# A gated linear recurrence in three passes of hi and lo weights instead of full fp32 matmuls, with its decay taken from an exponential

## The reference, cut to what matters

```python
def rglru_block(x, w_in, conv_w, conv_b, w_r, b_r, w_i, b_i, lam, w_out):
    gate, xr = jnp.split(x @ w_in, 2, axis=-1)
    xp = jnp.pad(xr, ((0, 0), (CONV_W - 1, 0), (0, 0)))
    xc = conv_b + sum(xp[:, k:k + S] * conv_w[k] for k in range(CONV_W))
    r = jax.nn.sigmoid(block_diagonal(xc, w_r) + b_r)     # 16 blocks of 80
    i = jax.nn.sigmoid(block_diagonal(xc, w_i) + b_i)
    log_a = -LRU_C * r * jax.nn.softplus(-lam)
    a = jnp.exp(log_a)
    u = jnp.sqrt(-jnp.expm1(2.0 * log_a)) * (i * xc)
    _, h = lax.associative_scan(_linear_recurrence_combine, (a, u), axis=1)
    return (h * jax.nn.gelu(gate)) @ w_out
```

## Time and profile before

| | |
|---|---|
| median of 3 runs | 1677.28 us (1676.93 to 1679.06) |
| the profiled execution | 1676.15 us |
| its span in the trace | 1674.4 us |
| granted TensorE clock, mean | 0.979 |
| PE busy | 1585.8 us, 95% |
| DVE, ACT busy | 778.7 us (47%), 505.6 us (30%) |
| instructions | 21914 |

### The profile page before, as it was taken

How to read it: one execution, slowest core, us unless ns; L and a number is a source line. 1 busy time by engine, 2 the same in 40 slices (tenths; PEclk the granted TensorE clock), 3 DMA queues, 4 the chain that set the end, 5 groups by cost and what they waited for, 6 DMA issues and landing times.

```text
span 1674.4 us, 21914 instructions
## 1 busy us (share of the span) xinstructions
PE 1585.8 (95%) x9206; PEld 1167.3 (70%) x9206; DVE 778.7 (47%) x1028; ACT 505.6 (30%) x573; POOL 61.4 (4%) x104
## 2 busy tenths in 40 slices
PE   8997999999999998999998899999999997899997
PEld 7745433333333337999896699998999986689997
DVE  1585411111111116545656665446554566574545
ACT  1241100000000003343354244343433435434332
POOL 2000000000000000000000000000000000000000
PEclk9997999999999999999999999999999998999999
DMA  9405899999999999753223369534854222179500
GB/s 312 142 1 245 362 414 428 429 428 429 428 428 429 429 395 369 253 193 108 76 72 131 126 225 365 189 127 150 284 194 152 100 69 83 51 273 348 182 0 26
DMA packets 149473, 395.27 MB, mean 236 GB/s; under 512 B 9458, under 2 KB 109936, under 8 KB 136608
## 3 DMA queue, kind: packets, MB, share of 16 engines
q1 hardware_dynamic: 146672, 385.67, 61.3%
q0 software_dynamic: 2736, 8.68, 1.5%
HBM read 393.28 MB, written 1.05 MB: 235 GB/s over the span
## 4 chain that ended last, share of the span: by engine, by line
PE 69%; DMA 14%; DVE 10%; issue 3%; ACT 3%; POOL 1%; SPq 0%; POOLq 0%; DVEq 0%; ACTq 0%
PE bank L1424 28%; DMA ring<-in_moe_w_dram 14%; PE bank L1437 12%; PE bank L894 8%; PE bank L650 3%; PE bank L923 2%; PE bank L703 2%; PE bank L1378 2%; PE bank L1453 1%; PE bank L911 1%; PE bank L1976 1%; PE bank L943 1%; PE bank L689 1%; DVE stats L545 1%; DVE x_tok L543 1%
## 5 line engine op out<-in xcount | busy, mean ns | idle before, releaser
L894 PE MATMUL bank<-ring,arena 128*64 128x512 f32 x928 | 228.3, 596 | 9.4 <-DMA ring<-in_moe_w_dram 9.4
L1424 PE MATMUL bank<-x_hi,split_u_hi 128*128 128x256 f32 x656 | 185.9, 283 | 0.0
L1424 PE MATMUL bank<-x_lo,split_u_hi 128*128 128x256 f32 x656 | 185.6, 283 | 0.0
L1424 PE MATMUL bank<-x_hi,split_u_lo 128*128 128x256 f32 x656 | 185.6, 283 | 0.0
L1424 PE MATMUL bank<-x_hi,split_g_lo 128*128 128x256 f32 x640 | 181.1, 283 | 0.0
L1424 PE MATMUL bank<-x_lo,split_g_hi 128*128 128x256 f32 x640 | 181.1, 283 | 0.0
L1424 PE MATMUL bank<-x_hi,split_g_hi 128*128 128x256 f32 x640 | 181.1, 283 | 0.0
L894 PEld LDWEIGHTS bank<-ring,arena 128*64 128x64 f32 x928 | 69.9, 137 | 145.6 <-issue 111.8
L1282 DVE TENSOR_TENSOR split_g_lo<-ring,split_g_hi 128x2048 fp32r<-128x2048 f32 x44 | 100.8, 2292 | 112.3 <-ACT split_g_hi L1276 112.3
L1124 DVE SCALAR_TENSOR_TENSOR arena<-arena,work 128x256 f32<-128x256 f32 x32 | 15.5, 484 | 287.7 <-PE bank L943 287.6
L1424 PEld LDWEIGHTS bank<-x_hi,split_u_hi 128*128 128x128 f32 x656 | 125.8, 192 | 0.5
(11 more groups left out here) (356 smaller groups left out, 2522.2 us busy)
## 6 DMA issues: line engine op xcount, KB each, us to landing
ring<-in_moe_w_dram SPq DMA_DIRECT2D x92, 2048.0 KB, 19.1
ring<-in_ffn_w_in_dram SPq DMA_DIRECT2D x88, 1024.0 KB, 8.9
ring<-in_ffn_w_out_dram SPq DMA_DIRECT2D x44, 1024.0 KB, 8.6
ring<-in_ml_w_in_dram SPq DMA_DIRECT2D x12, 1024.0 KB, 5.2
ring<-in_rec_w_in_dram SPq DMA_DIRECT2D x10, 1024.0 KB, 13.8
ring<-in_at_w_in_dram SPq DMA_DIRECT2D x6, 1024.0 KB, 5.2
ring<-in_rec_w_out_dram SPq DMA_DIRECT2D x5, 1024.0 KB, 9.9
gb_row<-in_ln_g_dram POOLq DMA_DIRECT2D x8, 512.0 KB, 6.9
```

The source lines that it names most:

```text
L894: i = nc.tensor.matmul(bank[4 + p][64 * j:64 * j + 64, :], xe[p][:, k, :], unit_view(n, 4)[:, k % 4, :], start=(k == 0), stop=(k == KT - 1))
L1424: i = nc.tensor.matmul(up_bank(kind, s_)[:, m * T:(m + 1) * T], w, xp_[b][:, k, :], start=(k == 0 and j == 0), stop=(k == KT - 1 and j == 2))
```

## The change

- **Three passes.** Unit 0 of `rec_w_in` stays fp32. The other 9, and the 5 of `rec_w_out`, are split to hi (ACT, L233 of the changed kernel) and lo (DVE, L238): 14 splits. x is split to `rx_hi`, `rx_lo`, and the rows of each group to `ry_hi` (ACT) and `ry_lo` (DVE).
- **Ring.** A unit that is split takes two slots, the second for its hi part. So the last three `rec_w_in` loads wait for `recA_used`, and the first expert's loads wait for it too instead of for `ln_in`.
- **Decay.** A new exponential of -2 times the old argument gives the decay less the reciprocal: DVE has no L824, L825 any more, and makes the decay and the root from the exponential by two scalar_tensor_tensor operations and one tensor_scalar.
- **Memory.** The transposed x is in `x_parts` at first, so half of the zeroing of `x_parts` comes after the first unit.
- Semaphores of the memory and attention layers are merged, and their counts shifted; nothing else of these layers changes.

```diff
@@ def columns(g, o), rec_pe
                 for k in range(KT):
-                    i = nc.tensor.matmul(o[:, b * T:(b + 1) * T], unit_view(n, KT)[:, k, b * P:(b + 1) * P],
-                                         xT[:, k, :], start=(k == 0), stop=(k == KT - 1))
+                    if g == 0:
+                        i = nc.tensor.matmul(to, w_in[:, k, at], xq[:, k, :], start=(k == 0), stop=(k == KT - 1))
+                        continue
+                    nc.tensor.matmul(to, w_hi[:, k, at], rx_hi[:, k, :], start=(k == 0), stop=False)
+                    nc.tensor.matmul(to, w_hi[:, k, at], rx_lo[:, k, :], start=False, stop=False)
+                    i = nc.tensor.matmul(to, w_lo[:, k, at], rx_hi[:, k, :], start=False, stop=(k == KT - 1))
...
-                pe.wait_ge(landed[n % RING], 16 * (n // RING + 1))
-                pe.wait_ge(r["y"], g + 1)
+                n = rec_out(g)
+                pe.wait_ge(w_lo_done, 2 * GROUPS + g)
+                pe.wait_ge(rec_lo_done, 3 + g)
@@ sync_program
+            for g in range(3 * GROUPS):
+                n = rec_in(g) if g < 2 * GROUPS else rec_out(g - 2 * GROUPS)
...
-                if n >= RING:
-                    sp.wait_ge(recA_used, n - RING + 1)
+                free_for(n)
...
                 sp.dma_start(dst, src).then_inc(landed[n % RING], 16)
+                if g > 0:
+                    free_for(n + 1)
+                    sp.sem_inc(landed[(n + 1) % RING], 16)
@@ rec_act
+            rec_split_act(act, 0)
+            rec_split_act(act, 1)
             for g in range(GROUPS):
...
+                for i in ((2,), (3, 4), (5,), (6, 7), ())[g]:
+                    rec_split_act(act, i)
...
+            rec_split_act(act, 8)
             for g in range(GROUPS + 2):
...
+                    if g < 2:
+                        rec_split_act(act, 9 + g)
+                if g >= 3:
+                    rec_y_act(act, g - 3)
                 if g >= 2:
...
+                        nc.scalar.activation(rec_b[q % 2][:, b, :], th_r[q % 2][:, b, :], ACT.Exp,
+                                             scale=lam_q[:, 4, nb:nb + 1], bias=lam_q[:, 4, nb:nb + 1])
...
-                    nc.scalar.activation(root[q % 2], th_r[q % 2], ACT.Sqrt).then_inc(r["sqrt"], 1)
+                    nc.scalar.activation(root[q % 2], th_r[q % 2], ACT.Sqrt, scale=0.25).then_inc(r["sqrt"], 1)
+                    if g < GROUPS:
+                        rec_split_act(act, 9 + g)
+            rec_y_act(act, GROUPS - 1)
+        def rec_y_act(act, q):
+            act.wait_ge(r["y"], q + 1)
...
+            nc.scalar.activation(ry_hi[q][:], gelu[:, 2 * q:2 * q + 2, :], ACT.Copy).then_inc(rec_hi_done, 1)
@@ rec_dve
+                    rec_split_dve(dve, 8 + g)
+                if g == GROUPS:
+                    rec_split_dve(dve, 13)
+                if g >= 3:
+                    rec_y_dve(dve, g - 3)
                 if g >= 2:
...
-                    own.then(nc.vector.tensor_scalar(rec_b[s], th_r[s], 1.0, None, ALU.add))
-                    own.then(nc.vector.reciprocal(rec_b[s], rec_b[s]))
...
-                    own.then(nc.vector.tensor_tensor(root[s], root[s], rec_b[s], ALU.mult))
-
-                    own.then(nc.vector.tensor_scalar(rec_b[s], rec_b[s], 2.0, -1.0, ALU.mult, ALU.add))
+                    own.did(nc.vector.scalar_tensor_tensor(out=root[s], in0=rec_b[s], scalar=1.0, in1=root[s],
+                                                           op0=ALU.add, op1=ALU.mult))
+                    own.then(nc.vector.scalar_tensor_tensor(out=th_r[s], in0=rec_b[s], scalar=1.0, in1=th_r[s],
+                                                            op0=ALU.add, op1=ALU.mult))
+                    own.did(nc.vector.tensor_scalar(th_r[s], th_r[s], -1.0, 1.0, ALU.mult, ALU.add))
```

More of the change, by code:

```diff
@@ L189, in build, with rec_hi, rec_lo, rec_split_act @@
         lam_q = sb("lam_q", [P, 12, CH])
+        xq = x_parts[:, 0:KT * T].rearrange("p (k t) -> p k t", k=KT)
+        rx_hi = nc.alloc_sbuf_tensor_at("rx_hi", [P, KT, T], F32R, offset=parts_at - KT * T * 4)
+        rx_lo = nc.alloc_sbuf_tensor_at("rx_lo", [P, KT, T], F32R, offset=h_at)
+        ry_lo = nc.alloc_sbuf_tensor_at("ry_lo", [P, CH, T], F32R, offset=arena_at + 8720 * 4)
+        ry_at = (work_at, arena_at + 11280 * 4, arena_at, arena_at + 520 * 4, work_at)
+        ry_hi = [nc.alloc_sbuf_tensor_at(f"ry_hi{q}", [P, 2, T], F32R, offset=at) for q, at in enumerate(ry_at)]
+        rec_hi_done, rec_lo_done = sem("rec_hi_done"), sem("rec_lo_done")
+        w_hi_done, w_lo_done = sem("w_hi_done"), sem("w_lo_done")
+        REC_W = 3 * GROUPS - 1
+        REC_SPLITS = [rec_in(g) for g in range(1, 2 * GROUPS)] + [rec_out(g) for g in range(GROUPS)]
+        def rec_hi(n):
+            return ring_r[:, (n + 1) % RING, :]
+        def rec_lo(n):
+            return ring_r[:, n % RING, :]
+        def rec_split_act(act, i):
+            n = REC_SPLITS[i]
+            act.wait_ge(landed[n % RING], 16 * (n // RING + 1))
+            act.wait_ge(landed[(n + 1) % RING], 16 * ((n + 1) // RING + 1))
+            nc.scalar.activation(rec_hi(n), unit(n), ACT.Copy).then_inc(w_hi_done, 1)
+        def rec_split_dve(dve, i):
+            n = REC_SPLITS[i]
+            dve.wait_ge(w_hi_done, i + 1)
+            nc.vector.tensor_tensor(rec_lo(n), unit(n), rec_hi(n).bitcast(F32), ALU.subtract).then_inc(w_lo_done, 1)
         mo = {n: sem("moe_" + n) for n in (
@@ L259, in sync_program, with free_for @@
                 sp.dma_start(x_tok[:, t, :], A["x"][0, t * P:(t + 1) * P, :]).then_inc(s_x, 16)
[L261 to L262 removed]
+            def free_for(n):
+                if n >= R0 + RING:
+                    sp.wait_ge(*rec_used(n - RING))
+            for slot in range(R0):
+                sp.sem_inc(landed[slot], 16)
+            for g in range(3 * GROUPS):
+                n = rec_in(g) if g < 2 * GROUPS else rec_out(g - 2 * GROUPS)
+                if g == 2 * GROUPS:
                     sp.wait_ge(s_wzero, 1)
@@ L731, in rec_act @@
                 act.wait_ge(s_xT0, b + 1)
-                nc.scalar.activation(xT[:, 2 * b:2 * b + 2, :], bank[b][:].rearrange("p (a t) -> p a t", a=2), ACT.Copy).then_inc(s_xT0b, 1)
+                nc.scalar.activation(xq[:, 2 * b:2 * b + 2, :], bank[b][:].rearrange("p (a t) -> p a t", a=2), ACT.Copy).then_inc(s_xT0b, 1)
+            act.wait_ge(s_xT0b, 4)
+            for j in range(2):
+                nc.scalar.activation(rx_hi[:, 4 * j:4 * j + 4, :], xq[:, 4 * j:4 * j + 4, :], ACT.Copy).then_inc(rec_hi_done, 1)
+            rec_split_act(act, 0)
+            rec_split_act(act, 1)
             for g in range(GROUPS):
```

176 lines of the change are left out of this document (105 added, 71 removed).

## The result

Over 20 executions of each, the changed kernel takes 1681.38 us (1677.47 to 1683.89) and the kernel before 1677.99 (1676.78 to 1679.26): ratio 1.0018, 95% interval 1.0011 to 1.0024, **3.4 us slower**. I forecast 1678.3 and held 1672 to 1686. A second series, of seven executions, gave 1681.63 against 1677.11, ratio 1.0027 (1.0015 to 1.0038). So the time lies in the range and the sign is right, but the difference is 3.4 to 4.5 us where I forecast 1.0: small, clear of the noise, and on the edge of what I had called "within 0.2%" or just past it.

A forecast was written before the change was run, and what follows sets the result against it. PE bounds the recurrent part before the change; afterwards late gates(0) and ACT-DVE turns do. Mark shift -2.6, half clock +2.9 on gates(0) and +0.7 on project 4 sum to +1.0 us: 1678.3 us, range 1672 to 1686.

The forecast's parts named there:

- within 0.2%: Outcome class for the whole kernel: a difference up to 3.4 us, not told from no change; chance 0.49.
- PE's saving of 17.9 us: Recurrent layer: nine rec_w_in units and five projects in three passes save 10.5 + 7.4 us if PE stays the bound.
- the two places named: Gates(0) starting late behind small loads and rec_w_out, 12.2 us PE idle; ACT and DVE taking turns, 11.9 us a group.
- the mark: Half of project 4, where the chain leaves PE: 138.45 us before, forecast 135.8 without clock loss, -2.6 us.
- Gates(0): First gates on PE, released by DVE's convolution of group 1: start forecast at 70.0 us, where it was 65.98.
- the start of the small loads: SyncE's 40 small loads behind the last rec_w_in load: forecast to start at 35.3 and end at 58.8 us.
- PE's own queue: PE's work from gates(3) at 99 us through project 3: forecast to end about 130.5, so PE waits for project 4.
- The turns: Recurrent groups: ACT's 7.4 us and DVE's 4.43 us alternate with two hand-overs, forecast period 11.9 us.
- what would have given 1689: A drain of about 1.38 us per ACT table switch, making the chain 11 us longer; the forecast rejected it.
- The clock: Half clock after PE idles: forecast +2.9 us on gates(0) and +0.7 on project 4.
- The early expert loads: First expert loads starting up to 30 us earlier: costed at nothing, gain bounded at about 7 us.
- spent on waiting: DVE's reciprocal in each group: its 3.36 us are saved on DVE but lost waiting in the turns with ACT.

The follow-up runs named there:

- e2: Changed kernel with the splits of rec_w_out moved behind the roots on ACT, DVE's lo parts moving with them: 1670.39 us, ratio 0.9950.
- e6: Changed kernel with the 40 small gate-weight loads issued on GpSimd's queue, with their own semaphore, instead of SyncE's: 1665.47 us, ratio 0.9923.
- e3: Changed kernel with the ry_hi copy and ry_lo subtraction of a group moved behind the next group's root and scans: 1679.49 us, ratio 1.0010.
- e5: Changed kernel with the first twelve expert loads held back until the norm after project 4 has started: 1679.51 us, ratio 1.0014.
- c1: Changed kernel run again with no edit, beside the kernel before: 1681.63 us, ratio 1.0027.
- e1: Changed kernel with 55 useless matmuls put ahead of PE's wait for gates(0), to keep its clock up: 1678.51 us, ratio 1.0004.
- e10: Changed kernel with the old decay (reciprocal on DVE, no exponential), so three passes, splits and paired slots alone: 1690.94 us, ratio 1.0086.
- e11: Kernel before with the exponential decay and its 40 small loads on GpSimd's queue, without three passes: 1675.98 us, ratio 0.9994.
- e9: e7 with the first twelve expert loads also held until the norm after project 4 has started: 1664.37 us, ratio 0.9921.
- e7: Changed kernel with the edits of e2, e3 and e6 together: 1664.5 us, ratio 0.9920.
- e8: Changed kernel with units 1 and 2 of the first projection also in fp32, unsplit like unit 0: 1679.02 us, ratio 1.0010.

## Why the prediction was right, and where it was off

*What binds.* Right. PE's saving of 17.9 us didn't come through at the two places named. e2 and e6 show the first, and e6 its price: the mark moved by 12.3 to 13.9 us, for 12.2 in the forecast. e3 shows the second.

*Gates(0).* 70.0 was forecast; 71.35 in the lucky profile, 72.7 to 74.3 in the others of the same form. Of the 1.35 us, 0.6 come from small loads that start at 35.90 instead of 35.3 and 0.7 from 24.2 us instead of 23.5 for issuing them. From there on the chain holds to 0.1 us: 5.1 us to landing, split, copy, convolution.

*The step that was off: the start of the small loads.* "the tightest, the lo part of unit 1, is ready at about 16.6 for 17.1, and even 2 us of delay there would only move the 34.8." The sum had the small loads at 35.3. They started at 35.90 in the first profile and at 37.6 to 39.6 in the six others of the form, so a term that was put at nothing is 0.6 to 4.3 us. Two things move it. In e3 and e5 PE waits for a lo part: ScalarE's split of unit 1 starts at 15.26 and 13.40 us for 12.52 in the first profile, that of unit 2 at 21.68 and 20.56 for 18.56, each time on a landing. With 4.2 us of splitting (1.91 + 2.29) between a landing and PE, nothing is left of a margin of 0.5 us that came from one execution. In c1, e1, e2 and e10 the first unit is still at half clock up to 14.5 to 15.3 us and takes 8.8 to 9.2 us, where the forecast ("unit 0 ends at 10.20 + 6.9") had it at full clock. The second half of the quoted sentence names the consequence and then drops it: the 34.8 is the start of the small loads, and so moves `rec_w_out`, gates(0) and the mark. The mark is 0.5 us behind that of the kernel before in the first profile, 2.1 in c1 and 2.4 in e5.

That this makes the medians is argued and not shown. c1's profiled execution is 3.2 us over the profiled one of before, but 2.3 under its own median; e5's mark is as late, and its profiled execution took 1676.74 us. And the slow first unit tells the two kernels apart only if it strikes one of them more often: e11 has it without three passes, at the same price of 2.2 us, and an execution without a trace doesn't say whether it had it. Part of the +3.4 and +4.5 thus has no shown cause.

*PE's own queue.* The forecast had it end at 130.5 us, 2.5 ahead of the last rows, so that PE would wait. It ended at 135.9, with the rows ready at 135.80. From gates(3) on it took 33.6 us for 31.3: 1.5 for gates(3) at half clock, 0.9 for projects of 5.65 to 5.68 us instead of 5.45. The forecast had seen the idle time before gates(3) and given it slack; the slack was used up to within 0.1 us. That this cost nothing was luck, and it is why e3 gains nothing.

*The turns.* Right: 11.86 us measured for 11.9. From the row of a table load and its successor nothing is added to a switch (0.02 us); what would have given 1689 didn't occur.

*The clock.* Mis-sized: +2.9 and +0.7 forecast, 1.6 to 1.8 and 0 measured, and nothing forecast for gates(3) and the first unit. The half clock of the windows starts at 61.2 us and lasts 13.7, so that ten of them pass while PE is idle; I had let it begin with gates(0). Project 4 ran at 1.00, because the idle time ahead of it didn't occur. With these 2 us less and gates(0) 1.35 later, the forecast mark (135.8 + 2.9 + 0.7 = 139.4) and the measured one (139.0) agree by errors that cancel.

*The early expert loads.* Right at nothing: they went out 27 us earlier, and neither e5 nor e9 shows them to give or to cost anything that these series can tell.

*The parts.* The forecast treated the exponential as saved on DVE and "spent on waiting". As a part of this change it was the one that kept the result near zero: without it, +13.8 us (e10).

The best version is e6's edit, one queue for another: 1665.47 us, 0.9923 of the kernel before; with the two other moves 1664.4 to 1664.5, which five executions each can't tell from it.

## What to carry to other kernels

A faster engine is worth what its next supplier allows: before pricing the passes, follow the release of the last buffer through the queue that refills it, and look at what else is issued in that queue ahead of the load that somebody waits for. Here 40 small starts, 0.6 us each, were hidden behind a slow PE and became the critical path with a fast one; moving them to an idle queue was worth about 1% (0.9923 for 1.0018 to 1.0027), more than any part of the change. A margin of half a microsecond that rests on one execution's landing is no margin: carry the delay through to the end of the chain before calling it harmless. And a clock of 1.00 in a view counts only where the trace has a record of it: the spacing of like matmuls told of a half clock that the column didn't.

## What I had not expected of the hardware

- TensorE stays at its lower clock for some time after its first matmul, and the time differs between executions: the first record of the full clock is at 8.8 to 10.0 us in six profiles and at 14.2 to 15.3 in eight (c1, e1, e2, e6, e7, e8, e10, e11), with the first matmul at 5.9 to 6.1 in all. The late rise makes eight to eleven matmuls of the first unit start 0.43 us apart instead of 0.22 and costs 1.7 to 2.4 us. What decides it stays open.
- Loads queued at the program's start in the same order land at different times: ScalarE's split of unit 1 began between 12.5 and 15.5 us and that of unit 2 between 18.2 and 21.7, in the ten profiles that split both.
- Forty small loads take 22.8 to 25.2 us to issue on SyncE's queue and 22.3 on GpSimd's.
